# One stage of a long kernel, the rwkv scan: half of its 64x64 products go across the array, its chain is spread over three units, and its state stays in PSUM

## The reference, cut to what matters

```python
def rwkv7_scan(r, w, k, v, a, b, state, reverse, with_out):
    def step(s, inp):
        rt, wt, kt, vt, at, bt = inp
        sa = jnp.einsum('bhij,bhj->bhi', s, at)
        s = s * wt[:, :, None, :] + sa[..., None] * bt[:, :, None, :] + vt[..., None] * kt[:, :, None, :]
        y = jnp.einsum('bhij,bhj->bhi', s, rt) if with_out else None
        return s, y
```

## Time and profile before

| | us |
|---|---|
| median of the runs (3624.53, 3626.92, 3631.2) | 3626.92 |
| the profiled execution, its own time | 3630.52 |
| its span from the first to the last instruction | 3628.7 |
| TensorE busy in the span | 3374.2 |
| the rwkv stage, first to last TensorE record of its products | about 782 |

### The profile page before, as it was taken

The page is one execution under the profiler, slowest core; times in us unless marked ns, Lnnn a source line. Parts: engine busy times, 40 slices in busy tenths (PEclk is TensorE's granted clock), DMA queues, the critical chain, the costliest instruction groups (busy, mean ns, idle before and its releaser), DMA issues. The chain is left out here.

```text
span 3628.7 us, 79113 instructions
## 1 busy us (share of the span) xinstructions
PE 3374.2 (93%) x35358; PEld 2634.2 (73%) x35358; DVE 1622.8 (45%) x3112; ACT 1152.1 (32%) x2433; POOL 403.9 (11%) x615
## 2 busy tenths in 40 slices
PE   7998998999999699899999999999989898899998
PEld 5767976788888568799999887788867676534343
DVE  3354455433333452367777675433344564211112
ACT  3343233322223332345555444322243333100001
POOL 0000122100000100222222221000011200100000
PEclk9999999999999899999999999999999999799999
DMA  4493153211111210000000001322111223499996
GB/s 184 141 357 126 47 226 117 93 70 47 70 70 52 85 47 24 9 6 6 5 13 5 28 5 41 121 97 93 70 68 51 81 76 139 208 403 411 414 428 289
DMA packets 35235, 437.39 MB, mean 121 GB/s; under 512 B 5024, under 2 KB 5632, under 8 KB 9168
## 3 DMA queue, kind: packets, MB, share of 16 engines
q1 hardware_dynamic: 29856, 414.10, 28.6%
q0 software_dynamic: 5040, 18.23, 1.6%
HBM read 425.49 MB, written 6.82 MB: 119 GB/s over the span
## 5 line engine op out<-in xcount | busy, mean ns | idle before, releaser
L758 PE MATMUL ps<-part 128*128 128x512 f32 (+1 forms) x4656 | 856.8, 346 | 43.4 <-DVE part L998 16.2
L758 PEld LDWEIGHTS ps<-part 128*128 128x128 f32 x4656 | 734.1, 194 | 162.3 <-issue 20.4
L2053 PE MATMUL ps<-part 128*128 128x512 f32 (+1 forms) x1536 | 549.3, 358 | 18.4 <-DVE part L2100 11.8
L2054 PE MATMUL ps<-part 128*128 128x512 f32 (+1 forms) x1536 | 548.6, 357 | 0.0
L2055 PE MATMUL ps<-part 128*128 128x512 f32 (+1 forms) x1536 | 548.4, 357 | 0.0
L3880 PE MATMUL ps<-part 128*64 128x512 f32 x1536 | 374.6, 608 | 27.9 <-DMA part<-in_wg 14.0
L2077 DVE TENSOR_TENSOR part<-part 128x1024 fp32r<-128x1024 f32 x128 | 158.7, 1240 | 495.3 <-ACT part L2066 495.3
L2477 PE MATMUL ps<-part 64*64 64x64 f32 x9984 | 340.6, 219 | 10.4 <-DVE part L2635 4.6
L2053 PEld LDWEIGHTS ps<-part 128*128 128x128 f32 x1536 | 289.8, 189 | 68.2 <-DVE part L2100 12.9
L2477 PEld LDWEIGHTS ps<-part 64*64 64x64 f32 x9984 | 315.5, 135 | 30.8 <-ACT part L2880 7.3
L2054 PEld LDWEIGHTS ps<-part 128*128 128x128 f32 x1536 | 290.3, 189 | 46.5
(11 more groups left out here) (419 smaller groups left out, 4320.4 us busy)
## 6 DMA issues: line engine op xcount, KB each, us to landing
part<-in_ada_w SPq DMA_DIRECT2D x36, 2048.0 KB, 9.6
part<-in_mlp_w SPq DMA_DIRECT2D x32, 2048.0 KB, 7.6
part<-in_wg SPq DMA_DIRECT2D x32, 2048.0 KB, 14.3
part<-in_wu SPq DMA_DIRECT2D x32, 2048.0 KB, 13.2
part<-in_wd SPq DMA_DIRECT2D x32, 2048.0 KB, 14.0
part<-in_b_in SPq DMA_DIRECT2D x8, 2048.0 KB, 7.5
part<-in_ab_w_in SPq DMA_DIRECT2D x7, 2048.0 KB, 8.0
part<-in_rkv SPq DMA_DIRECT2D x6, 2048.0 KB, 7.4
```

Of the source, the lines that this page charges most:

```text
L758: mm = pe.e.matmul(ps[:, j * n:j * n + n], lhs, rhs, start=k == ks[0] and i == 0, stop=k == ks[-1] and i == 2)
L2053: pe.e.matmul(ps, wh[:, k, :], hi[:, k, x0:x1], start=k == 0, stop=False)
L2054: pe.e.matmul(ps, wh[:, k, :], lo[:, k, x0:x1], start=False, stop=False)
```

## The change

It rewrites the rwkv stage's schedule; the arithmetic stays the same up to the order of sums.

- **Crossed and straight.** `gram`, `blocks` and `turned` get an argument `flip`. With 1, a head's output goes to the other half of the partitions (`half(hd ^ flip)`), so its product uses the rows of one half and the columns of the other. Gram, X turned, P X, XT M, rh, uu and y are crossed; squares, X add, M XT, ka, br, bk and zz are straight. In a turn TensorE first issues all its straight products, then all its crossed ones (`for work in (straight(c, turn), crossed(c, turn)): together(work)`). The `yield`s set no order where only one generator runs.
- **Three units.** In cycle c TensorE does the first half of the solve of unit c + 1 (gram to X add 1), the second half of the solve of unit c (from X add 2 on, with ka, br, bk), and the stream of unit c - 1; prep is split over units c + 2 and c + 1. There is one cycle more.
- **Both directions in one bank.** X add, X turned, P X, XT M, M XT, br, the last squares, rh, uu, zz and y of the two directions share a bank; X, XT, M, Arb, RH, UU are evicted for both in one instruction. Gram, squares 0 and 1, ka, bk stay one bank a direction.
- **State in PSUM.** zz begins with an identity product of zm; ScalarE evicts it with the gain as its scale, one instruction a direction. L2749, L2753 and L2985 go.
- **Order on ScalarE and VectorE.** ScalarE's stream evictions stand first in each turn, then Pf, NP, XT and BK, then prep (the tanh at turn 4), keys, end. VectorE has X and XT in turn 5, the masks of ka in turn 6.
- y is added for the two directions in two half instructions, which also put the heads back; tensors are laid out anew, me and gn have four buffers.

```diff
-PREP = {1: 0, 3: 1, 4: 2, 5: 3, 6: 4, 7: 5, 8: 6, 9: 7}
+PREP_FIRST = {4: 0, 6: 1, 8: 2, 9: 3, 11: 4}
+PREP_LAST = {0: 5, 1: 6, 2: 7}
...
+def rw_clock():
+
+    for c in range(-2, UNITS + 2):
         for turn in range(TURNS):
...
+            yield c, turn
...
+def together(*works):
+
+    works = list(works)
+    while works:
+        for work in list(works):
+            if next(work, "done") == "done":
+                works.remove(work)
...
+    def right_hand(n, sub):
+
+        bank = K.bank("rh", n, sub)
+        for u in both(K, n):
...
+            for hd, o in halves():
+                mm = pe.e.matmul(ps[half(1 - hd)], u.A[o, g, 0, :], r.V[u.m % 2][o, x, :], start=True, stop=first,
+                                 skip_group_check=True)
...
+    def states(n, sub):
+
+        if not following(n, sub):
+            return
+        bank = K.bank("zz", n, sub)
+        pe.wait_ge(K.at("BK", n))
...
+            if not first:
+                for hd, o in halves():
+                    pe.e.matmul(ps[o], K.ident[o, o], r.zm[sub % 2][o, u.d, :], start=True, stop=False, skip_group_check=True)
+                yield
+            for hd, o in halves():
+                pe.e.matmul(ps[o], u.BK[o, 1, g, :], r.V[u.m % 2][o, x, :], start=first, stop=False, skip_group_check=True)
+            yield
+            pe.wait_ge(K.at("uu in", n, sub))
+            for hd, o in halves():
+                mm = pe.e.matmul(ps[o], u.BK[o, 0, g, :], r.UU[sub % 2][o, u.d, :], start=False, stop=True,
+                                 skip_group_check=True)
...
+    def crossed(c, turn):
+
+        n = c + 1
+        if turn == 4 and here(n):
+            for u in both(K, n):
+                pe.wait_ge(K.at("made", *u.key))
+                ps = K.bank("gram", *u.key).rearrange("p (g x c) -> p g x c", g=4, x=2)
+                yield from gram(ps[:, :, 1:2, :], u, u.aa, u.ops[:, 1:2, :], 1)
+                yield from gram(ps[:, :, 0:1, :], u, u.bb, u.ops[:, 0:1, :], 1, ("gram", *u.key))
+        n = c
+        if turn == 3 and here(n):
+            pe.wait_ge(K.at("X", n, 3))
+            ps = K.bank("X turned", n)
...
+        if turn in (3, 7) and here(n):
...
+            ps = K.bank(("PX", lev), n)
...
+        if turn in (5, 9) and here(n):
...
+            ps = K.bank(("XM", lev), n)
...
+            sub, part = divmod(turn, 3)
+            yield from (right_hand, solution, outputs)[part](n, sub)
+
+    def straight(c, turn):
+
+        n = c
+        if turn == 1 and here(n):
...
+            ps = K.bank(("X add", 2), n)
...
+        if turn == 3 and here(n):
+            for u in both(K, n):
                 ps = K.bank("bk", *u.key)
...
+        if turn == 4 and here(n):
+            for u in both(K, n):
+                ps = K.bank("ka", *u.key).rearrange("p (g x c) -> p g x c", g=4, x=2)
...
+        if turn == 5 and here(n):
+            ps = K.bank("XMT", n)
...
+        if turn == 7 and here(n) and n % 3:
+            ps = K.bank("br", n).rearrange("p (d g x c) -> p d g x c", d=2, g=4, x=1)
...
+        n = c + 1
+        if turn in (8, 10) and here(n):
+            lev = turn // 2 - 4
+            pe.wait_ge(K.at("NP", n, lev + 1), K.at("X", n, lev))
+            ps = K.bank(("X add", lev), n)
...
+        if turn in (6, 8) and here(n):
...
+                if turn == 8 and u.d == 0 and here(c - 1):
+                    yield from states(c - 1, 2)
+        if turn == 10 and here(n):
+            ps = K.bank(("squares", 2), n)
...
+        if turn % 3 == 2 and here(c - 1) and not (turn == 8 and here(c + 1)):
+            yield from states(c - 1, turn // 3)
+
+    for c, turn in rw_clock():
+        step, n = prep_at(c, turn)
+        if step == 0:
+            for u in both(K, n):
+                ps = K.bank("lora", *u.key)
...
+        for work in (straight(c, turn), crossed(c, turn)):
+            together(work)
...
+            v.e.tensor_tensor(four(r.X[n % 3]), four(r.X[n % 3]), K.ps.of(("XM", 1), n), ADD).then_inc(
+                *v.up(("X", n, 4), free(("XM", 1), n)))
+            v.wait_ge(K.at("XT", n, 1))
+            v.e.tensor_tensor(four(r.XT), four(r.XT), K.ps.of("XMT", n), ADD).then_inc(
+                *v.up(("XT", n, 2), free("XMT", n)))
+        if turn == 6 and here(n):
...
+                v.wait_ge(K.at("ka", *u.key))
+                v.e.tensor_tensor(u.A.rearrange("p g x c -> p g (x c)")[:, :, 0:w],
...
+            if part == 1:
+                s.wait_ge(K.at("uu", n, sub), K.at("streamed", *previous(n, sub, 2)) if 4 * n + sub >= 2 else {})
+                s.e.activation(r.UU[sub % 2].rearrange("p d c -> p (d c)"), K.ps.of("uu", n, sub)[:, 0:128],
+                               ACT.Copy).then_inc(*s.up(("uu in", n, sub), free("uu", n, sub)))
+            if part == 2 and to:
...
+                    s.e.activation(r.zm[to[1] % 2][:, u.d, :], K.ps.of("zz", n, sub)[:, 64 * u.d:64 * u.d + 64], ACT.Copy,
+                                   scale=w.gain(to[1])).then_inc(*s.up(("zm", *to), free("zz", n, sub)))
```

More of the change, by code:

```diff
@@ L2516, in rw_pe @@
-            if turn == 11:
-                if u.lat:
-                    ps = K.bank("br", *u.key)[:, 0:256].rearrange("p (g x c) -> p g x c", g=4, x=1)
-                    gram(u, ps, u.bb, u.ops[:, 3:4, :]).then_inc(*pe.up(("br", *u.key)))
+                yield from gram(ps[:, :, 1:2, :], u, u.aa, u.ops[:, 1:2, :], 1)
[4 more added lines that the diff above has]
+            ps = K.bank("X turned", n)
+            for u in both(K, n):
+                yield from turned(ps, 256 * u.d, [u.X[:, g, :] for g in range(4)], 1, *([("X turned", n)] if u.d else []))
@@ new lines, in crossed @@
+        n = c - 1
+        if here(n):
+            for _ in range({1: 4, 6: 8, 8: 12, 10: 8}.get(turn, 0)):
+                yield
+            sub, part = divmod(turn, 3)
[3 more added lines that the diff above has]
+        if turn == 1 and here(n):
+            pe.wait_ge(K.at("NP", n, 3), K.at("X", n, 2))
+            ps = K.bank(("X add", 2), n)
+            for u in both(K, n):
+                yield from blocks(ps, 256 * u.d, u.NP[:, 1], u.X, 0, *([(("X add", 2), n)] if u.d else []))
+        if turn == 3 and here(n):
+            for u in both(K, n):
@@ new lines, in rw_dve @@
+        step, m = keys_at(c, turn)
+        kk = r.kk[m % 2]
+        if step == 0:
+            if m >= 2:
+                v.wait_ge(*[K.at("tmp used", d, 3 * m - 4) for d in range(2)])
+            v.e.tensor_scalar(kk, a.kT[:, m, :], kkv[:, m:m + 1], None, MUL).then_inc(*v.up(("kk raw", m)))
+        if step == 3:
+            for j, (x0, x1) in enumerate(BOTH):
+                v.wait_ge(K.at("norms", m, j))
+                v.e.tensor_scalar(r.sq[:, x0:x1], K.ps.of("norms", m, j)[:, 0:x1 - x0], 1e-24, None, MAX).then_inc(
+                    *v.up(("kk sum", m), free("norms", m, j)))
@@ new lines, in rw_act @@
+        if step == 5:
+            if m >= 2:
+                s.wait_ge(K.at("streamed", 3 * m - 4))
+            for j, (x0, x1) in enumerate(BOTH):
+                s.wait_ge(K.at("v turned", m, j))
+                s.e.activation(r.V[m % 2].rearrange("p x c -> p (x c)")[:, x0:x1], K.ps.of("v turned", m, j)[:, 0:x1 - x0],
+                               ACT.Copy).then_inc(*s.up(("v rows", m), free("v turned", m, j)))
+        step, m = end_at(c, turn)
+        if step is None:
+            continue
@@ L2942, in rw_pool @@
         weights(d, 0)
-    for n in sorted(K.rw.cn):
-        K.load(pool, K.rw.cn[n], K.const_src(n), "rw const", n)
-    for what, turn, u in rw_turns(K):
-        if what == "prep":
+    for n in sorted(r.cn):
+        K.load(pool, r.cn[n], K.const_src(n), "rw const", n)
+    for c, turn in rw_clock():
+        step, n = prep_at(c, turn)
+        for u in both(K, n) if step is not None else ():
             s = u.s
             sg, B, av, e2, kd = s.tmp
-            r = a.rT[:, u.m, u.lo:u.hi]
-            if turn == 3:
+            rr = a.rT[:, u.m, u.lo:u.hi]
+            if step == 3:
                 if u.b == 2 and u.m < 7:
```

852 lines of the change are left out of this document (414 added, 438 removed).

## The result

The changed kernel takes 3757.32 us (median of four runs, 3755.08 to 3764.15) against 3628.3 us before: a ratio of 1.0353, with an interval from 1.0336 to 1.0369. That is 129 us slower. The forecast was 62 us slower, so the direction was right, but the forecast size was less than half of the measured one, and 3757 us lies outside the range that ends at 3745. The profiled execution took 3764.15 us, with a span of 3762.4.

The account below looks back on a forecast made before the run. TensorE was taken as the bound, busy 88.16 of 90.80 us in the stage. Terms -49 + 19 - 13 + 0 + 111 = +68 us, taken as +62, gave 3689 us; own range 3650 to 3730, whole range 3590 to 3745.

Parts of the forecast that it names:

- (a): Turn 5: zz waits for a bank freed by ScalarE's late tanh evictions, 0.9 us a cycle, table loads apart.
- (b): Turn 5: y, or the squares in its place, waits for the ka masks VectorE does in turn 6, 2.2 us.
- (c): Turns 2 and 11: the states wait for UU with little work between, 0.8 us a cycle together.
- (d): Once in three cycles: table load ahead of the tanh, 1.3 us; keys' load, logarithms and exponentials ahead of UU, 1.5 us.
- second rival: PSUM bank rings: evictions get done under other work, so 111 becomes 40 and the kernel takes 3618 us; chance 0.12.
- What it newly waits for: New TensorE waits from PSUM bank order and late evictions: 111 us over 22 full cycles, bounds 30 to 150.
- part 4: Solve and stream spread over three units: operands ready earlier, about 1.6 idle us per three units go, -13 us.
- Part 1: Crossed and straight products on TensorE overlap at changes of kind, 0.17 us each: 49 us gained.
- third rival: Crossed and straight products do not overlap at 64 columns: +49 us more, 3738 us; chance 0.15.
- first rival: TensorE's queue reaches past a whole run, so the two kinds run together: about 3597 us; chance 0.20.
- Part 2: State kept in PSUM: 640 identity-product records at 29 ns add 19 us on TensorE, all on the path.
- Part 3: Joined evictions: some 20 us of VectorE's work go, nothing on the path.

Follow-up runs that it names:

- e12_fill16: Changed kernel with 16 idle 128-column products put on TensorE in front of the norms' wait, no wait removed: 3747.1 us.
- three moves: Changed kernel with ka masks at the start of turn 5, tanh ahead of UU, keys' square from k and keys' product in turn 3: 3637.3 us.

## Why the prediction was wrong

**Direction: right, by its own mechanism.** (a) was to cost 0.9 x 22 plus the table loads, some 29 us, and its idle time is 29.7; (b) was 2.2 x 22 = 48 us, and is 44; (c) was 0.8 x 22 = 18, and is 20.4. Of (d), the table load is there (2.4 us instead of 0.9 in one of three waits for the tanh), but no row shows the 1.5 us before UU in the keys' cycle, 11 us in all. The rings and the fixed orders of ScalarE and VectorE did what the count said, so the second rival (they don't bite) and the fourth are out.

**The term that was mis-sized: "What it newly waits for", +111 us.** It priced a wait at its idle time, and the clock behind it at nothing, without a reason. The runs show that (b) was worth 70 us, (a) 48, and all three moves 120. Most of the difference is the granted clock: it falls to 1.2 GHz behind such idle times, and that lengthened TensorE's busy time in the stage by some 37 us against before. e12_fill16 shows it by filling one of the waits. The rows of before had the clock at 1.00 in the three units of the earlier trace rows; nothing in the working asked whether it would stay there once 2 us holes came in every unit.

**The step that failed outright: "the norms' wait stays (ScalarE and VectorE do the same there)", in part 4.** The wait for the norms' eviction, which the earlier trace rows shows, did stay (4.6 us in the stage before, 5.6 after). What grew is the wait of the norms themselves for the keys' square, from 3.2 to 25.5 us. ScalarE and VectorE do the same, but GpSimd doesn't: its products moved from turns 7 and 8 of a cycle to turns 0 and 1, beside the keys' product, which went from 0.6 to 6 us. The prediction counted queues in the order of their own instructions and never laid VectorE's against GpSimd's in time. Taking the square off the product and the product away from there brought 19 us, most of it busy time and clock.

**Part 1, -49 us.** Measured -38 on the changed kernel and -42.5 on the three moves: a little less than 12 changes of kind at 0.17 us. The estimate of -14, with starts 25 ns apart, is out; so is the third rival (no overlap), although its 3738 us came nearest to the measured time. The first rival (a queue that reaches past a whole run) is out for runs. Its arithmetic, four quarters at once, is real when the kinds alternate, but its 158 us did not come: on the three moves alternating gave 20 us, with 68 us of pauses for instructions.

**Part 2, +19 us:** 12 on the three-move kernel. **Part 3:** VectorE's busy time in the stage fell only from 521 to 506 us, where some 60 were to go (20 here and the 40.6 of L2749); the held keys' product took 33 of them back. **Part 4, -13 us, and the ends, 0:** not tested by themselves.

Together, idle and busy time apart: the forecast's waits less part 4 are 111 - 13 = 98 us of idle time, and with the norms' 22 it is 120; the stage has 157.5 - 38 = 119.5. Busy time by the measured terms is the clock's 37, crossing's -38 to -42.5 and the identity products' 12, between 6.5 and 11 us; the stage has 740.5 - 731 = 9.5. The agreement is better than the single terms deserve, since several are off by some us in both directions, and the two experiments' terms were taken on other kernels or executions.

## What to carry to other kernels

Price a new wait on TensorE by its idle time and by what the clock does behind it; here each microsecond of wait cost about 1.6 for (a) and (b), and 1.5 for the three moves together. When a step is moved, lay the queues of VectorE and GpSimd side by side in time, and keep long SBUF-to-SBUF operations of the one away from unbroken runs of the other. Spreading small products over four quarters pays only where they stand next to each other in the queue, and only until the instructions themselves run out, here one block of 256 in 3.5 to 4.0 us.

## What the runs showed of the hardware

- VectorE's 128x768 operation from SBUF to SBUF took 6.01 us (one source) and 6.42 us (two sources) beside eight GpSimd operations in a row, and 0.61 us elsewhere. GpSimd's own stayed at 0.71 us each.
- Products 64x64x64 in float32, alternated over four quarters, start every 14.8 ns within a block; over 2048 of them the mean is 27.1 ns, with pauses of 1.38 to 1.92 us at every 256th instruction.
- In runs of a kind, products of the other two quarters begin only at the joint; that was worth 38 to 42.5 us over the stage, alternating the kinds 75 us on the same kernel.
- Sixteen useless products in a wait of 4 us made the kernel 10 us faster: around the norms at 1758 us the granted clock stayed at 2.4 GHz, where the changed kernel had stretches at 1.2 GHz.
